# Recurrent stage of a hybrid decoder layer: the last three operations of the group norm run in the next pair

## The reference, cut to what matters

```
y = jnp.moveaxis(ys, 0, 1)
mu = jnp.mean(y, axis=-1, keepdims=True)
var = jnp.mean(jnp.square(y - mu), axis=-1, keepdims=True)
yn = ((y - mu) * lax.rsqrt(var + GN_EPS)).reshape(B, T, W) * lnx_w + lnx_b
bonus = jnp.sum(r_h * k_h * r_k, axis=-1, keepdims=True) * v_h
out = (yn + bonus.reshape(B, T, W)) * g
```

## Time and profile before

| | |
|---|---|
| time, median of 3 runs | 2415.04 us (2414.31 to 2415.66) |
| time of the profiled execution | 2415.23 us |
| its span | 2413.5 us |
| TensorE busy | 2351.0 us (97%) |
| VectorE busy | 1473.5 us (61%) |
| ScalarE busy | 879.6 us (36%) |
| chain that ended last | PE 82%, DVE 10%, issue 4%, ACT 1% |

### The profile page before, as it was taken

The page is one execution under the profiler, slowest core; times in us unless marked ns, Lnnn a source line. Parts: engine busy times, 40 slices in busy tenths (PEclk is TensorE's granted clock), DMA queues, the critical chain, the costliest instruction groups (busy, mean ns, idle before and its releaser), DMA issues.

```text
span 2413.5 us, 48839 instructions
## 1 busy us (share of the span) xinstructions
PE 2351.0 (97%) x19616; PEld 2252.7 (93%) x19616; DVE 1473.5 (61%) x2125; ACT 879.6 (36%) x1048; POOL 131.3 (5%) x203
## 2 busy tenths in 40 slices
PE   8999999999999999999999998999999999999999
PEld 6899989898888888888999988999999999999998
DVE  5644544566677666776535457665666666566676
ACT  6443344343332233322434344333333333333334
POOL 3000011000000010000001010000000000000003
PEclk9999999999999999999999999999999999999999
DMA  7554487342333243332445633444444444444443
GB/s 267 185 165 142 160 285 251 97 140 90 99 100 96 85 137 96 100 96 86 151 153 160 197 105 105 157 140 143 158 151 149 147 156 140 143 157 151 152 145 110
DMA packets 282189, 346.67 MB, mean 144 GB/s; under 512 B 6957, under 2 KB 240733, under 8 KB 280907
## 3 DMA queue, kind: packets, MB, share of 16 engines
q1 hardware_dynamic: 271883, 307.66, 39.6%
q0 software_dynamic: 9712, 36.30, 4.5%
q10 hardware_dynamic: 464, 0.79, 0.1%
HBM read 333.83 MB, written 10.89 MB: 143 GB/s over the span
## 4 chain that ended last, share of the span: by engine, by line
PE 82%; DVE 10%; issue 4%; ACT 1%; DMA 1%; DVEq 1%; SPq 0%; ACTq 0%
PE bank L246 19%; PE bank L255 19%; PE bank L247 19%; PE bank L227 4%; PE bank L229 4%; PE bank L228 4%; PE bank L1193 3%; DVE work L911 2%; ACT hi L211 1%; DVE lo L218 1%; PE bank L1210 1%; PE bank L511 1%; DVE work L1025 1%; PE bank L512 1%; PE bank L518 1%
## 5 line engine op out<-in xcount | busy, mean ns | idle before, releaser
L218 DVE TENSOR_TENSOR lo<-raw,hi 128x2048 fp32r<-128x2048 f32 x286 | 655.8, 2293 | 502.9 <-ACT hi L211 485.6
L246 PE MATMUL bank<-ah,hi 128*128 128x320 f32 x3200 | 957.4, 313 | 0.2 <-DVE al L532 0.2
L247 PE MATMUL bank<-al,hi 128*128 128x320 f32 x3200 | 945.9, 309 | 0.0
L211 ACT ACTIVATE hi<-raw 128x2048 fp32r<-128x2048 f32 x286 | 548.0, 1916 | 935.1 <-PE bank L255 681.1
L246 PEld LDWEIGHTS bank<-ah,hi 128*128 128x128 f32 x3200 | 601.0, 188 | 15.4 <-issue 13.3
L247 PEld LDWEIGHTS bank<-al,hi 128*128 128x128 f32 x3200 | 601.4, 188 | 0.4
L255 PE MATMUL bank<-ah,lo 128*128 128x320 f32 x3200 | 545.4, 311 | 2.5 <-DVE lo L218 2.5
L255 PEld LDWEIGHTS bank<-ah,lo 128*128 128x128 f32 x3200 | 486.4, 188 | 7.4 <-DVE lo L218 4.1
L227 PE MATMUL bank<-bh,hi 128*128 128x320 f32 x704 | 218.7, 311 | 0.2 <-DVE work L2410 0.2
L229 PE MATMUL bank<-bh,lo 128*128 128x320 f32 x704 | 217.5, 309 | 0.0
L228 PE MATMUL bank<-bl,hi 128*128 128x320 f32 x704 | 217.5, 309 | 0.0
(11 more groups left out here) (386 smaller groups left out, 2090.7 us busy)
## 6 DMA issues: line engine op xcount, KB each, us to landing
raw<-in_w_in SPq DMA_DIRECT2D x98, 1024.0 KB, 5.3
raw<-in_w_up SPq DMA_DIRECT2D x88, 1024.0 KB, 5.1
raw<-in_w_down SPq DMA_DIRECT2D x44, 1024.0 KB, 5.1
raw<-in_w_branch SPq DMA_DIRECT2D x24, 1024.0 KB, 5.5
raw<-in_w_out SPq DMA_DIRECT2D x16, 1024.0 KB, 5.4
raw<-in_w_mem_k SPq DMA_DIRECT2D x8, 1024.0 KB, 5.8
raw<-in_w_mem_v SPq DMA_DIRECT2D x8, 1024.0 KB, 5.2
work<-in_cache_mem_k POOLq DMA_DIRECT2D x8, 1024.0 KB, 6.0
```

The source lines that it names most:

```text
L211: act.activation(hi[c % NS][:, :], raw[c % 2][:, :], ACT.Copy).then_inc(S("hi_done"), 1)
L218: dve.tensor_tensor(lo[c % NS][:, :], raw[c % 2][:, :], hi[c % NS][:, :], ALU.subtract)\
L246: pe.matmul(out, w, xh[:, 8 * h + k, :], start=h + k == 0, stop=False)
L247: pe.matmul(out, w, xl[:, 8 * h + k, :], start=False, stop=False)
```

## The change

The three last operations of the norm become `norm_out(dve, vv, i)` and run in pair i on the values of pair i-1, behind the sum for `t_rt` and ahead of the copies of A2 and B2. In pair 0 they run on constants set ahead of the loop, and after pair 7 once more in `branch_dve`. The normed rows lie one row further. The tiles change so that values can live longer: `ym` in `ka_t`, `ysq` in `t_x`, and ScalarE copies "bonus" to `t_ck`, at once and no longer behind `gated_out`; VectorE's product of bonus and v therefore stands before the evictions of BCt and BCs. ScalarE waits for `gated_out` before its copies of vkt instead. `weights_low(5)` stands ahead of the last `branch`, the copy of y ahead of `prepare_rest`, and ScalarE takes the root after it has passed the wait for "tr0".

```
-        y_, ym, ysq = t_x, zc[:, 0:T], zc[:, T:2 * T]
+        y_, ym, ysq = t_x, ka_t, t_x
+        def norm_out(dve, vv, j):
+            dve.wait_ge(S("gn_root"), j + 1)
+            vv.do(dve.reciprocal(ysq, ysq))
+            vv.do(dve.tensor_tensor(ym, ym, ysq, ALU.mult))
+            vv.do(dve.tensor_tensor(row_(j), ym, bon, ALU.add), "gated_out")
...
                 tt(c5(t_rt), c5(t_ad), bmid(m_id[:, :], NC), ALU.add)
+                norm_out(dve, vv, i)
                 plain(t_a2, "A2")
                 plain(t_b2, "B2")
+                dve.wait_ge(S("turned_out"), OUT0_A + N_OUT_A * i + OUT_A["bonus"] + 1)
+                tt(bon, t_ck, row_(i + 16), ALU.mult)
...
                 plain(t_bd, "B4")
-                dve.wait_ge(S("turned_out"), OUT0_A + N_OUT_A * i + OUT_A["bonus"] + 1)
-                tt(bon, bon, row_(i + 16), ALU.mult)
...
-                prepare_rest(dve, vv, i + 1)
                 dve.wait_ge(S("y_ps"), i + 1)
                 vv.do(dve.tensor_copy(y_, bank[6][:, 0:T]), "y_out")
+                prepare_rest(dve, vv, i + 1)
...
                 prepare_ops(dve, vv, i + 1)
+                weights_low(5)
                 branch(1, 1)
-                dve.wait_ge(S("gn_sqrt"), i + 1)
-                vv.do(dve.reciprocal(ysq, ysq))
-                tt(ym, ym, ysq, ALU.mult)
-                tt(row_(i), ym, bon, ALU.add, "gated_out")
-                weights_low(5)
...
                 ps("bonus")
-                act.wait_ge(S("gated_out"), j)
-                aa.do(act.activation(bon, pbank("bonus")[:, 0:T], ACT.Copy), "turned_out")
+                aa.do(act.activation(t_ck, pbank("bonus")[:, 0:T], ACT.Copy), "turned_out")
                 act.wait_ge(S("wkv_ps"), PS0 + NPR * i + PR["ssq"] + 1)
                 aa.do(act.activation(sq, pbank("ssq")[:, 0:T], ACT.Sqrt), "kk_root")
+                act.wait_ge(S("gated_out"), j + 1)
...
-                ps("mean")
+                ps("tr0")
                 act.wait_ge(S("ring_out"), OUT0 + N_OUT * j)
-                aa.do(act.activation(ysq, ysq, ACT.Sqrt), "gn_sqrt")
+                act.activation(ysq, ysq, ACT.Sqrt).then_inc(S("gn_root"), 1)
+                act.wait_ge(S("gn_root"), j + 1)
...
-            act.wait_ge(S("gated_out"), KW + 1)
-            aa.do(act.activation(bh[:, :, :], rw[:, 0:KW, 0:T], ACT.Copy), "bh_ready")
+            act.wait_ge(S("gated_out"), KW + 2)
+            aa.do(act.activation(bh[:, :, :], rw[:, 1:KW + 1, 0:T], ACT.Copy), "bh_ready")
...
         def branch_dve(dve, vv):
+            norm_out(dve, vv, KW)
```

More of the change, by code:

```diff
@@ L869, in wkv_start_dve @@
             vv.do(dve.memset(st_[0], 0.0), "ring_out")
+            vv.do(dve.memset(ym, 0.0))
+            vv.do(dve.memset(bon, 0.0))
+            vv.do(dve.memset(ysq, 1.0), "gn_root")
             vv.do(dve.memset(st_[1], 0.0), "gated_out")
@@ L1097, in wkv_act @@
         def wkv_act(act, aa, n):
-            with aa.loop(4 * n, 4 * n + 4, {"act": 2, "low_out": 2, "exps": 3, "kk_root": 1, "v_copied": 1, "gn_sqrt": 1, "turned_out": N_OUT_A}) as i:
+            with aa.loop(4 * n, 4 * n + 4, {"act": 2, "low_out": 2, "exps": 3, "kk_root": 1, "v_copied": 1, "turned_out": N_OUT_A}) as i:
                 units = [0]
@@ L1351, in wkv_pe @@
                 wait("sam_ready", i + 1)
-                wait("gated_out", i + 1)
+                wait("gated_out", i + 2)
                 sam_, vtm_ = [x.rearrange("p b v -> p (b v)") for x in (sam, vtm)]
@@ L1916, in branch_dve @@
         def branch_dve(dve, vv):
+            norm_out(dve, vv, KW)
             dve.wait_ge(S("bh_ready"), 2)
-            vv.do(dve.tensor_tensor(bl[:, :, :], rw[:, 0:KW, 0:T], bh[:, :, :], ALU.subtract), "bl_ready")
+            vv.do(dve.tensor_tensor(bl[:, :, :], rw[:, 1:KW + 1, 0:T], bh[:, :, :], ALU.subtract), "bl_ready")
             with vv.loop(8, 11, {"gate_free": 4}) as i:
```

## The result

| | before | changed |
|---|---|---|
| median | 2415.35 us (4 runs, 2414.31 to 2418.65) | 2437.53 us (4 runs, 2435.79 to 2439.44) |
| profiled execution, its span | 2415.23 us, 2413.5 us | 2439.44 us, 2437.4 us |
| mean granted TensorE clock | 0.996 | 0.986 |
| TensorE busy | 2351.0 us | 2365.3 us |

The changed kernel takes 22.2 us more. The ratio is 1.009, 95% interval 1.0072 to 1.0107. The direction was forecast with 0.85, the time lies 7 us above the forecast of 2430.5 and 1.5 us above the range.

The account below looks back on a forecast made before the run. TensorE, busy 97% of the span, was taken as the bound. Seven places +6.4, pair 0 +3.8 and the end -0.8 gave +9.4; with +6.0 for the clock, 2415.04 became 2430.5 us, range 2421 to 2436.

Parts of the forecast that it names:

- The two waits are one: Between pairs: TensorE's 1.3 us waits at beCt and BCt share one cause; time saved at beCt is waited at BCt.
- End of a pair: With the norm gone and lo earlier, VectorE idles 0.5 us before ABt's first eviction; the wait for hi costs nothing.
- bonus copy: At beCt: the copy no longer waits for the norm, so TensorE saves the 1.28 us wait there.
- copy of y: Ahead of `prepare_rest`: TensorE's 0.3 us wait goes, a head start of 0.3 us at each later place.
- The first part of a pair: Norm before A2's copy: one 3.2 us wait at BCt, vkt 0.92 us later; +6.4 us over seven places.
- Pair 0: First pair, norm run on constants: +3.8 us, with a wait of 3.3 us at BCt.
- After pair 7: After the last pair: the 2.48 us wait for lo goes, a 3.5 us wait for hi comes; -0.8 us.
- The clock: TensorE's clock falls behind long waits in six of eight pairs and at the end; +6.0 us.
- More than forecast: Rival: the clock falls everywhere and its loss isn't taken up before vkt; +22.9 us, 2438; chance 0.06.
- The clock holds: Rival: small products around the wait keep TensorE's clock up; 2424.4 us; chance 0.27.
- Faster: Rival: the 1.28 us saved at beCt isn't given back at BCt; 2403 us; chance 0.06.
- the norm is hidden: Rival: VectorE starts ABt's evictions at once and the bonus product falls into idle time; 2419.3 us, no change; chance 0.09.

Follow-up runs that it names:

- e5: Kernel before with only the bonus copy and root of ssq freed from waiting for the norm, which stays at the pair's end; 2417.57 us, ratio 1.0.
- e3: Whole computation, built from the kernel before, with the norm's three operations late in the next pair, between additions of Z2 and Z3; 2393.51 us, ratio 0.9907.
- e1: Changed kernel with five extra TensorE products, results overwritten, in the wait at BCt; 2425.8 us, ratio 1.004.
- e2: Changed kernel with the norm's reciprocal replaced by a plain copy, so normed rows differ from the reference; 2411.09 us, ratio 0.9978.
- e7: Changed kernel with two extra TensorE products, results overwritten, in the wait at BCt; 2428.24 us, ratio 1.0048.
- e9: Changed kernel as it stands, measured again beside the kernel before; 2437.14 us, ratio 1.009.
- e4: e3 with the norm's three operations moved ahead of the copy of A2, nothing else; 2440.12 us, ratio 1.0099.
- e6: Kernel before with the last unit's lo ahead of the branch sum and norm, and hi ahead of the root; 2439.26 us, ratio 1.0095.

## Why the prediction was wrong, point by point

**The two waits are one, set by VectorE's row of work.** Right, but for where the wait goes. e5 takes one away without a gain, and e3 takes the norm out of the row and wins both. But in e5 TensorE waited at A2, for the eviction of ABs, and not longer at BCt. In the change, where VectorE is free before ABt, the whole wait stands at BCt.

**End of a pair, bonus copy, copy of y.** Right: no wait for the root or the copy of y, 0.56 us of idle time before ABt's first eviction, `hi` ahead in time.

**The first part of a pair.** Right in mechanism, and nearly in size. The wait at BCt was given as 3.2 us and is 3.6: TensorE gets from the bonus product to A2 in 5.55 us, 0.3 less than I had, and the rest is a tenth here and there. Without the clock (e1) a pair takes 75.8 to 76.1 us from bonus to bonus, 0.4 to 0.8 us more than before, against +0.92. The sum was read from pair 2, where TensorE waited 0.2 us before vkt. In the kernel before it waited there in every pair, and 0.3 to 0.6 us in pairs 4 to 7:

```profile
PE bank L1210 <- DVE work L911: 2.3, 8, 0.6
```

So less came on top there.

**Pair 0.** Right: +3.8 was given; e1 has 76.1 us to the next pair against 72.4.

**After pair 7.** Right in the wait (3.5 given, 3.6 measured). In e1 it takes 0.3 us more than before from the bonus product of pair 7 to the first `bh` product, where 0.92 - 0.8 = +0.1 was given. From the bonus product of pair 0 to that point e1 takes 7.9 us more than before, so the sum of +9.4 without the clock was 1.5 us too high.

**The clock** is the step that failed. It said: "I take the nearer row, that it falls, in six of the eight pairs and at the end", and "0.75 stays: 6 x 0.75 + 1.5 = +6.0". Two sizes in it were off. It fell in eight of eight. And a fall was priced by one row, a fall of 3.4 us that cost 1.5 us. For that length the 0.75 was near: 0.6 to 0.7 us in pairs 1, 4 and 7, 0.5 to 0.8 in e2 and e7. But five of the eight lasted 6.8 us, and of so long a fall the wait before vkt takes up little: TensorE itself became the last there (VectorE idle for 1.52 us at RT1), and each cost 1.5 to 2.0 us. From BCt to vkt the mean is 7.30 us against 5.95 with the clock held, 1.3 us per pair and 10.8 in all, where 4.5 was given. The fall at the end cost 2.4 us, where 1.5 was given. In sum the clock took 13.2 us of the profiled execution and not 6.0. The trace of the kernel before held two more such rows, far behind the pairs, which the prediction left out. On PE, and the windows behind:

```profile
1435.17 0.52 PE L477 MATMUL bank<-ident,rw 128*128 128x128 f32 x3 [3.60 <-DVE mix L2070]
1456.10 0.60 PE L2135 MATMUL bank<-ah,hi 128*128 128x320 f32 x1 [5.57 <-DVE al L2075]
...
1436.70:1440.00 3.30, 3.30 (x10) 2.30 (x10) 3.09 (x7) 1.88 (x4) 2.99 (x5) 0.50 0.00 0
1453.80:1460.50 6.70, 4.40 (x17) 4.43 (x17) 6.35 (x11) 2.95 (x4) 0.00 (x0) 0.50 0.00 1
```

The clock fell at both waits, and at the one of 5.57 us it was at half for 6.8 us, from 2.4 us before TensorE resumed. So a long fall could have been read ahead of the change.

A single fall can thus cost more than the bound of 1.5 us, though the mean in the pairs doesn't. The range ended at 2436 because it took in only half of the higher case. The rule of the Trainium skill (TensorE: Matmul & The Clock Gate, section HAM oscillation), that a wait in every turn of a loop can bring the clock down in every turn, is what the trace shows, eight times; it was set aside for "six of eight".

**The rivals.** *More than forecast*, at 2438 with a chance of 0.06, gave the measured time, and nearly for its reason: the clock falls everywhere, and its loss is not taken up. In part it is luck: its row of work is 1.5 us too high, and its 9 x 1.5 = 13.5 us for the clock comes near 13.2 though no fall cost just that. Its chance was too small: at each of the three waits of 2.48, 3.60 and 5.57 us in the trace of the kernel before the clock had fallen. *The clock holds* is e1, 9.7 us over the kernel before against 9.4 given, of which 1.6 are the fall after pair 7. *Faster* and *the norm is hidden* were not to be had from this place, but a place 30 us later in the pair gives more than the faster rival's 2403.

## What to carry to other kernels

When an operation is moved off one wait, follow the busy row of its engine to the next point where somebody waits: as long as the operation stayed in that row, nothing was won here, and 7.9 us were lost even with the clock held; it has to go where the engine is idle, even if its values must be kept longer. A wait of TensorE should be priced with what the clock does behind it, and by its length in one piece: two waits of 1.3 us with 5 us of work between cost 2.6, one of 3.6 us cost 4.9 in the mean. Where such a wait can't be removed, TensorE work in it that nobody needs can pay.

## What the hardware showed that was not expected

How long a wait must be for the clock to fall is no fixed figure in these runs. After seven waits of 1.3 us at BCt in the kernel before: none. In e5, with a second one 1.5 us earlier: one of seven. After 1.75 to 2.04 us (e2): five of eight, all 3.4 us long. After 2.2 to 2.5 us (e7): six of eight, all 3.4 us long. After 3.6 to 3.9 us (the change): eight of eight, five of them 6.8 us long, and the same in e9; e4 and e6, with waits of 3.7 to 4.1 us, have 15 of 15, ten of them 6.8 us long. The fall can begin while TensorE is busy again: in e2 it began 0.8 to 1.6 us behind the end of the wait. For pair 2 of e2, in which the wait ended at 708.38:

```profile
708.38:709.70 1.32, 1.32 (x43) 1.25 (x44) 0.96 (x2) 1.32 (x1) 0.00 (x0) 1.00 0.06 12
709.75:713.10 3.35, 3.35 (x15) 3.35 (x14) 2.93 (x5) 0.03 (x1) 0.00 (x0) 0.50 0.00 0
```

The waits of e2 were alike within 0.03 us from pair 1 to pair 7 but for one, and the fall came in some and not in others; what decides between them was not settled.
